# Value transposes behind the first Q strip, and the last two attention units interleaved, in a hybrid GDN, sliding-window attention and mixture-of-experts layer

## What is computed

```python
h = x @ w_in                      # 512 x 2048 by 2048 x 5648
a_qkv, a_z, a_beta, a_dec, b_q, b_k, b_v = jnp.split(h, SPLITS, axis=-1)
o_a = gated_delta_rule(...)       # 8 GDN heads of 128
# attention: 16 query heads of 64 on 4 key/value heads; a chunk of 64 queries
# sees its own chunk of keys and the one before
s = jnp.einsum('bnqhgd,bnkhd->bhgnqk', qc, kb) * (d ** -0.5)
s = s - slopes[:, :, None, None, None] * dist
s = jnp.where(valid, s, -jnp.inf)
p = jax.nn.softmax(jnp.concatenate([s, sink], -1), axis=-1)[..., :-1]
o = jnp.einsum('bhgnqk,bnkhd->bnqhgd', p.astype(v.dtype), vb)
mix = jnp.concatenate([o_a, o_b.astype(x.dtype)], -1) @ w_o
```

## Time and profile before

| | us |
|---|---|
| median of 3 runs | 2172.26 |
| the profiled execution | 2169.26 |
| its span, first to last instruction | 2167.3 |
| TensorE busy | 1920.7 (89% of the span) |
| VectorE busy | 1179.5 (54%) |
| ScalarE busy | 583.2 (27%) |
| GpSimd busy | 397.3 (18%) |
| mean granted TensorE clock | 0.959 |

### The profile page before, as it was taken

The page is one execution under the profiler, slowest core; times in us unless marked ns, Lnnn a source line. Parts: engine busy times, 40 slices in busy tenths (PEclk is TensorE's granted clock), DMA queues, the critical chain, the costliest instruction groups (busy, mean ns, idle before and its releaser), DMA issues.

```text
span 2167.3 us, 23945 instructions
## 1 busy us (share of the span) xinstructions
PE 1920.7 (89%) x9724; PEld 1208.9 (56%) x9724; DVE 1179.5 (54%) x1808; ACT 583.2 (27%) x875; POOL 397.3 (18%) x301
## 2 busy tenths in 40 slices
PE   4799999999999899699979998988998899898981
PEld 3687877787787777588853443433333333343330
DVE  6676577567657255411365554545555454454558
ACT  4233224224314255411222222122122112212211
POOL 1643233324233222144300000000000000000002
PEclk9899999999999999799979999999999999999995
DMA  5421222122113121152679999999999999999981
GB/s 194 155 78 40 59 59 59 42 57 66 52 40 85 52 66 59 64 181 97 238 267 403 403 405 407 411 398 403 406 415 408 398 414 402 398 413 404 412 352 78
DMA packets 170847, 505.89 MB, mean 233 GB/s; under 512 B 16336, under 2 KB 108624, under 8 KB 117232
## 3 DMA queue, kind: packets, MB, share of 16 engines
q1 hardware_dynamic: 167552, 491.61, 59.6%
q0 software_dynamic: 2608, 8.53, 1.4%
q10 hardware_dynamic: 576, 4.19, 0.5%
HBM read 499.97 MB, written 12.71 MB: 237 GB/s over the span
## 4 chain that ended last, share of the span: by engine, by line
PE 47%; DMA 33%; DVE 14%; ACT 2%; issue 2%; POOL 1%; SPq 1%; DVEq 0%; ACTq 0%
DMA ring<-in_w_up 32%; PE bank L1646 8%; PE bank L2004 8%; PE bank L1648 8%; PE bank L1647 8%; PE bank L2013 3%; PE bank L1777 2%; PE bank L1774 2%; PE bank L1766 2%; DVE half L1128 2%; PE bank L1973 1%; DVE gd_L L1249 1%; DVE att L1306 1%; DVE sc L1301 1%; DVE sc L1318 1%
## 5 line engine op out<-in xcount | busy, mean ns | idle before, releaser
L2004 PE MATMUL bank<-ring,xbT 128*64 128x512 f32 x2048 | 484.6, 616 | 78.8 <-DMA ring<-in_w_up 76.6
L599 POOL TENSOR_TENSOR wlo<-raw,whi 128x512 fp32r<-128x512 f32 x244 | 341.0, 1431 | 636.8 <-ACT whi L710 413.9
L1517 DVE TENSOR_TENSOR r<-r,bank 128x512 f32<-128x512 f32 x512 | 318.0, 681 | 211.1 <-PE bank L1973 210.6
L2004 PEld LDWEIGHTS bank<-ring,xbT 128*64 128x64 f32 x2048 | 156.8, 141 | 360.5 <-issue 358.3
L1646 PE MATMUL bank<-hTh,wlo 128*128 128x512 f32 x720 | 306.3, 425 | 21.9 <-POOL wlo L599 21.9
L1648 PE MATMUL bank<-hTh,whi 128*128 128x512 f32 x720 | 283.8, 394 | 0.0
L1647 PE MATMUL bank<-hTl,whi 128*128 128x512 f32 x720 | 283.3, 393 | 0.0
L987 ACT ACTIVATE yw<-bank,wts_all 64x512 f32<-64x512 f32 x256 | 174.8, 683 | 252.8 <-PE bank L2013 248.8
L2013 PE MATMUL bank<-ring,hidT 128*64 128x512 f32 x1024 | 228.5, 599 | 0.5 <-ACT hidT L980 0.5
L646 POOL DMA_INDIRECT xb<-h_scr,idx_tok x32 | 29.8, 931 | 885.6 <-PE bank L1980 871.7
L1973 PE MATMUL bank<-yhl,place 128*128 128x512 f32 x512 | 158.9, 430 | 11.9 <-DVE r L1517 9.1
(11 more groups left out here) (312 smaller groups left out, 2163.1 us busy)
## 6 DMA issues: line engine op xcount, KB each, us to landing
ring<-in_w_gate SPq DMA_DIRECT2D x128, 1024.0 KB, 28.4
ring<-in_w_up SPq DMA_DIRECT2D x128, 1024.0 KB, 29.0
ring<-in_w_down SPq DMA_DIRECT2D x128, 1024.0 KB, 28.2
raw<-in_w_in SPq DMA_DIRECT2D x45, 1024.0 KB, 5.6
raw<-in_w_o SPq DMA_DIRECT2D x16, 1024.0 KB, 5.2
xt<-in_x SPq DMA_DIRECT2D x4, 1024.0 KB, 9.3
h_scr<-xt SPq DMA_DIRECT2D x4, 1024.0 KB, 7.6
r<-h_scr SPq DMA_DIRECT2D x1, 4096.0 KB, 13.7
```

The source lines that it names most:

```text
L599: i = pool.tensor_tensor(wlo[sl][:, part, :], raw[sl][:, :].rearrange("p (k n) -> p k n", k=KD)[:, part, :], whi[sl][:, part, :].bitcast(F ...
L1517: dve.tensor_tensor(v, v, comb_bank(q, tt)[:, :], ALU.add).then_inc(comb_done, 1)
L2004: i = mm(GU[SLOTS * h:SLOTS * (h + 1), :], xT_[:, k, :], w[:, kk * F:(kk + 1) * F], start=k == 0, stop=k == KD - 1)
```

## The change

Two places.

**The head.** TensorE runs the first query strip (`k_steps(Q0, ...)`) ahead of the eight value transposes instead of behind them; the second strip stays behind them.

**The tail.** The functions of a unit are cut into pieces. Units 0 to 5 call them in the old order. Unit 7 gets its own score buffer `sc_last` (in the last 8 KB of `hTl`, so DVE waits for the last strip's matmuls, `strip_mm`), its own `att8_last`, and for r = 0 the banks `PA[0]`, `PA[1]`, which no strip needs any more. So TensorE issues both units' scores, and DVE and ACT take the first half of unit 7 between unit 6's exponentials and its normalisation. New waits: unit 7's scores of r = 1 wait until DVE has read unit 6's from the same bank (`sc_step`), and unit 6's value product, which writes `B2`, waits until DVE has read unit 7's scores there. The value product of every unit also names `at_out`. On ACT the split of block 0 moves from between the units to ahead of both.

```diff
@@ -190,6 +190,8 @@
+        sc_last = at("sc_last", HT + 56 * KB, [P, 2, 2, 2, 2 * P])
+        att8_last = at("att8_last", ATT + 28 * KB, [P, 5, 8])
...
@@ -456,6 +458,19 @@
+        UNITS = 8
+
+        def sc_of(u):
+            return sc_last if u == UNITS - 1 else sc
+
+        def att8_of(u):
+            return att8_last if u == UNITS - 1 else att8
+
+        def score_bank(u, r, tp):
+            if r == 0:
+                return PA[tp] if u == UNITS - 1 else [B0, B1][tp]
+            return [B2, BM][tp]
+
...
@@ -858,24 +873,33 @@
-            def attend(m, j):
-
-                u = 2 * m + j
-                for r in range(2):
...
-                                           accum_out=att8[:, 2, 4 * r + t:4 * r + t + 1])
-                i.then_inc(pexp, 1)
+            def exps(u, r):
+                j, a8 = u % 2, att8_of(u)
+                act.wait_ge(nmx, 2 * u + (r + 1))
...
+                if r == 1:
+                    i.then_inc(pexp, 1)
+
+            def turned(u):
                 for i in range(4):
                     act.wait_ge(pt_ps, 4 * u + (i + 1))
+            def mixed(u):
                 act.wait_ge(at_ps, u + 1)
-                act.activation(mixT[:, bass.ds(u + HEADS, 1), :].rearrange("p o s -> p (o s)"), B2[:, :],
-                               ACT.Copy).then_inc(at_out, 1)
+                act.activation(mixT[:, u + HEADS, :], B2[:, :], ACT.Copy).then_inc(at_out, 1)
+
+            def attend(m, j):
+                u = 2 * m + j
+                for r in range(2):
+                    exps(u, r)
+                turned(u)
+                mixed(u)
 
...
@@ -907,11 +931,17 @@
-            attend(3, 0)
             act.wait_ge(strip_mm, STRIPS)
             act.wait_ge(at_out, 4)
             split_mix(0)
-            attend(3, 1)
+            exps(6, 0)
+            exps(6, 1)
+            exps(7, 0)
+            turned(6)
+            exps(7, 1)
+            mixed(6)
+            turned(7)
+            mixed(7)
             for i in range(1, 3):
...
@@ -1285,49 +1315,59 @@
-            def attend(m, j):
-
-                u = 2 * m + j
-                if j == 0:
-                    W(dve, at_ps, 2 * m)
-                    dve.tensor_copy(kg[:, :], kdup[:, bass.ds(m, 1), :].rearrange("p o s -> p (o s)"))
-                    dve.tensor_copy(vg[:, :, :], vtok[:, :, bass.ds(m * HD, HD)])
-                    dve.tensor_copy(sl[:, :, :], attn_small[:, :].rearrange("p (a h) -> p a h", a=2)[:, :, bass.ds(m * 4, 4)]).then_inc(at_small, 1)
+            def group(m):
                 dve.wait_ge(at_small, m + 1)
-                W(dve, pt_ps, 4 * u)
-                for r in range(2):
-                    for tp in range(2):
-                        dve.wait_ge(sc_ps, 4 * u + (2 * r + tp + 1))
-                        dve.scalar_tensor_tensor(out=sc[:, r, tp, :, :], in0=dist[:, tp:tp + 2, :],
-                                                 scalar=sl[:, 0, 2 * j + r:2 * j + r + 1],
-                                                 in1=[[B0, B1], [B2, BM]][r][tp][:, :].rearrange("p (a b) -> p a b", a=2),
...
+
+            def biased(u, r):
+                j, a8 = u % 2, att8_of(u)
+                if r == 0 and u < UNITS - 1:
+                    W(dve, pt_ps, 4 * u)
+                for tp in range(2):
+                    dve.wait_ge(sc_ps, 4 * u + (2 * r + tp + 1))
+                    dve.scalar_tensor_tensor(out=sc_of(u)[:, r, tp, :, :], in0=dist[:, tp:tp + 2, :],
+                                             scalar=sl[:, 0, 2 * j + r:2 * j + r + 1],
+                                             in1=score_bank(u, r, tp)[:, :].rearrange("p (a b) -> p a b", a=2),
...
+            def normed(u):
+                a8 = att8_of(u)
                 dve.wait_ge(pexp, u + 1)
-                dve.tensor_tensor(att8[:, 4, :], att8[:, 2, :], att8[:, 3, :], ALU.add).then_inc(inv_sum, 1)
...
+                dve.reciprocal(a8[:, 4, :], a8[:, 4, :]).then_inc(inv_sum, 1)
                 dve.wait_ge(inv_sum, 2 * u + 2)
                 for r in range(2):
                     for tp in range(2):
-                        dve.tensor_tensor(sc[:, r, tp, :, :], sc[:, r, tp, :, :],
-                                          att8[:, 4, c:c + 2].rearrange("p (a o) -> p a o", o=1).broadcast_to([P, 2, 2 * P]),
+                        dve.tensor_tensor(sc_of(u)[:, r, tp, :, :], sc_of(u)[:, r, tp, :, :],
+                                          a8[:, 4, c:c + 2].rearrange("p (a o) -> p a o", o=1).broadcast_to([P, 2, 2 * P]),
                                           ALU.mult).then_inc(pn, 1)
...
-            attend(0, 0)
-            attend(0, 1)
-            for m in range(1, 3):
-                attend(m, 0)
-                attend(m, 1)
-            attend(3, 0)
-            attend(3, 1)
+            for u in range(UNITS - 2):
+                if u % 2 == 0:
+                    group(u // 2)
+                biased(u, 0)
+                biased(u, 1)
+                normed(u)
+            group(3)
+            biased(6, 0)
+            biased(6, 1)
+            dve.wait_ge(strip_mm, STRIPS)
+            biased(7, 0)
+            normed(6)
+            biased(7, 1)
+            normed(7)
...
@@ -1811,44 +1851,59 @@
+            k_steps(Q0, slot(0), 0, KD)
             for j in range(2):
                 pe.wait_ge(strip_out, Q0 - 1 + j)
                 pe.wait_ge(o_done, HEADS)
                 for t in range(TT):
                     i = pe.transpose([B0, B1][j][:, t * P:(t + 1) * P], vT[:, j, t * P:(t + 1) * P], ident)
                 i.then_inc(v_T, 1)
-            for j in range(2):
-                k_steps(Q0 + j, slot(j), 0, KD)
-
-            def attend(m, j, feed):
-                u = 2 * m + j
-
-                pe.wait_ge(at_small, m + 1)
+            k_steps(Q0 + 1, slot(1), 0, KD)
+
+            def scores(u):
+                j = u % 2
+                pe.wait_ge(at_small, u // 2 + 1)
                 pe.wait_ge(strip_out, u + (Q0 + 1))
-                W(pe, at_out, u)
+                if u < UNITS - 1:
+                    W(pe, at_out, u)
                 for r in range(2):
                     q0, q1 = HD * r, HD * (r + 1)
                     for tp in range(2):
+                        if u == UNITS - 1 and r == 1:
+                            pe.wait_ge(sc_step, 8 * (u - 1) + (5 + 2 * tp))
                         for t in (2 * tp, 2 * tp + 1):
-                            i = mm([[B0, B1], [B2, BM]][r][tp][:, (t % 2) * 2 * P:(t % 2 + 1) * 2 * P],
+                            i = mm(score_bank(u, r, tp)[:, (t % 2) * 2 * P:(t % 2 + 1) * 2 * P],
                                    aq[j][q0:q1, t * P:(t + 1) * P], kg[q0:q1, t * P:(t + 2) * P], start=True, stop=True)
                         i.then_inc(sc_ps, 1)
-                feed(13)
+
+            def turn(u):
                 for r in range(2):
                     pe.wait_ge(pn, 4 * u + (2 * r + 2))
                     for g in range(2):
                         for t in range(TT):
...
-                feed(2)
+
+            def weigh(u):
                 pe.wait_ge(pt, 4 * u + 4)
+                if u == UNITS - 2:
+                    pe.wait_ge(sc_step, 8 * (u + 1) + 5)
+                W(pe, at_out, u)
                 for t in range(TT):
                     for g in ((0, 1) if t else (1,)):
                         for r in range(2):
...
+
+            def attend(m, j, feed):
+                u = 2 * m + j
+                scores(u)
+                feed(13)
+                turn(u)
+                feed(2)
+                weigh(u)
                 feed(KD)
...
@@ -1866,8 +1921,11 @@
-            for j in range(2):
-                attend(3, j, lambda n: None)
+            for u in (6, 7):
+                scores(u)
+            for u in (6, 7):
+                turn(u)
+                weigh(u)
```

More of the change, by code:

```diff
@@ L859, in _ @@
             iteration(HEADS, last=True)
+            def exps(u, r):
+                j, a8 = u % 2, att8_of(u)
+                act.wait_ge(nmx, 2 * u + (r + 1))
+                act.activation(a8[:, 3, 4 * r:4 * r + 4], a8[:, 1, 4 * r:4 * r + 4], ACT.Exp,
+                               bias=sl[:, 1, 2 * j + r:2 * j + r + 1])
+                for t in range(TT):
+                    v = sc_of(u)[:, r, t // 2, t % 2, :]
+                    i = act.activation(v, v, ACT.Exp, bias=a8[:, 1, 4 * r + t:4 * r + t + 1],
+                                       accum_out=a8[:, 2, 4 * r + t:4 * r + t + 1])
+                if r == 1:
+                    i.then_inc(pexp, 1)
+            def turned(u):
+                for i in range(4):
+                    act.wait_ge(pt_ps, 4 * u + (i + 1))
+                    act.activation(pT[:, i, :], [BS, BO, B0, B1][i][:, :], ACT.Copy).then_inc(pt, 1)
+            def mixed(u):
+                act.wait_ge(at_ps, u + 1)
+                act.activation(mixT[:, u + HEADS, :], B2[:, :], ACT.Copy).then_inc(at_out, 1)
             def attend(m, j):
@@ new lines, in group @@
```

(18 more changed lines are left out.)

19 lines of the change are left out of this document (1 added, 18 removed).

## The result

The changed kernel took 2149.08 us (median of 4 runs, 2148.18 to 2151.27) beside 2171.72 for the kernel before (4 runs, 2169.8 to 2172.45). The profiled execution took 2148.52, its span 2146.5.

What follows compares the result with a forecast made beforehand. TensorE holds 47% of the chain, DMA 33%, VectorE 14%; TensorE idles at head and tail. Head 8.3 plus tail 8.9 is 17.2 us: 2169.26 becomes 2152.1, plus 3.0 to the median gives 2155.1, range 2150.5 to 2160.

Steps and rivals of the forecast that it cites:

- the head: From the last GDN matmul to unit 0's scores: TensorE goes straight on, scores at 750.3 instead of 758.64, 8.3 us gained.
- The covers: At the head, time to spare before TensorE needs its inputs: 7.7 us (copies, queries), 3.6 (second strip), about 6 (third strip).
- the chain of the two units: Tail, units 6 and 7: unit 7's transposes at 887.9 instead of 896.84, 8.9 us earlier.
- the projection's cold start: Output projection's first 4.0 us at half rate, worth 2.0 us; taken as unchanged, possibly 0.5 better to 1.5 worse.
- the first rival: Tail: full clock returns in unit 6 and stays, the projection starts warm; 4.4 us more, 2150.7 us; chance 0.13.
- the base: Profiled execution of the kernel before, 2169.26 us, from which the gain was subtracted; the median of its runs lies 3.0 above.
- The sum: Head 8.3 plus tail 8.9 us, 17.2 us gained; chance 0.72.
- the failed step: Tail, unit 7's transposes to the output projection: unchanged at 8.31 us, if the clock is at half as before.
- The other rivals: Head's gain absorbed, 2163.4 us (0.10); projection stays at half clock, 2191 (0.03); expert DMAs start at their own time, 2172.3 (0.02).
- The rule on transposes: Skill's claim that transposes don't engage full clock; by it unit 7's chain stays at half clock and the gain at 17.2 us.

Runs made afterwards that it cites:

- the second profile: The changed kernel once more, unaltered, against the kernel before: 2151.09 us (median of 5 runs), ratio 0.9908.
- fillers: Extra matmuls, results unused: 30 after the scores of units 6 and 7 each in the kernel before, 2165.23 us; 33 in the changed kernel, 2149.74 and 2148.35 us.

## Why the prediction was right and where it failed

**Right: the head.** "8.3 us" for unit 0's scores was 8.35. That it fits to 0.1 is partly luck: against the four profiles with the old head the same gain is 7.6 to 8.5, by how long the clock stayed at half there. The clock stayed full, as taken. The covers were there: queries at 742.1 (742.6 forecast), the third strip's split over at 746.7 (747), both before 749.97.

**Right: the chain of the two units.** From DVE's first step of unit 6 to unit 7's transposes 19.35 us, forecast 887.9 − 868.20 = 19.7. The split of block 0 was hidden: ACT's first exponential still waited 0.36 us for DVE, forecast 0.3. Unit 6's transposes came 11.07 us after DVE's first step (11.3), and the extra semaphores cost nothing that shows (109.54 us between the head and unit 6, 109.56 before).

**Failed: "From there on nothing changes: 905.15 − 896.84 = 8.31 us to the output projection, if the clock is at half as before", and with it the projection's cold start, "I take it as it was".** In two of three profiles the section took 5.48 us and the projection began warm, 2.83 + 1.85 = 4.7 us less. This is the first rival, put at 4.4 us and given a chance of 0.13. The argument against it was that the clock had stayed at half between 896.84 and 909.1 "although TensorE was mostly busy". That stretch began with a clock already down, after an idle of 8.53 us; in the changed kernel the two units' bursts are 2.17 us apart, and in those two profiles the clock that had returned behind unit 6's transposes was still there. The short gap alone does not secure it: in the second profile, with a gap of 2.37 us, the clock fell again at 881, and 7.38 us went by to a cold projection. What does secure it is work in the gaps: with fillers in both units the clock stayed at 1.00 in all three profiles. Why one execution keeps the clock and the next does not stays open. The row for the return, 881.8 in the earlier trace rows, had been read, and the step was still carried over from the old kernel.

**Also mis-sized: the base.** The sum was made against one execution whose tail was 2.9 us shorter than that of the next profile, because its clock came back earlier (881.7 instead of 911). The 3.0 us from that profile to the median were carried over to the changed kernel as a constant. The changed kernel's profile lies only 0.6 us under its own median (1.4 under that of the ten runs). Part of the 3.0 was perhaps half-clock work in unit 6 that the change hides; the executions without a profile cannot show it.

**How the miss adds up.** Forecast 2155.1, measured 2149.1, 6.0 us. Up to the first expert load the profile gained 22.66 where the sum had 17.2: 4.7 are the clock of the failed step, 0.4 the chain (9.29 for 8.9), 0.3 the stretch before the head. The longer expert stage took back 1.9. The base gave 3.0 − 0.6 = 2.4. Rounded, that is the 6.0. The lower end of the range, 2150.5, stood only 0.2 under the rival's 2150.7, so that any further gain beside the rival left it.

**The other rivals** did not occur: the head alone gave 9.0 us, so it was not absorbed; the first load followed the projection; and the projection was at full clock from its start or from 4.4 us on.

**The rule on transposes.** At 881.8, before, the clock rose during unit 6's transposes, and TensorE had done nothing else since 878.68; at 874.7, after, it rose 0.4 us behind them. The Trainium skill (TensorE: Matmul & The Clock Gate, section on PE-mode transposes) says that full rate "doesn't engage" for transposes; by it neither rise was to be expected. The traces disagree: unit 7's sixteen took 2.30 us at a granted clock of 1.00, unit 6's at half 3.68. The page measured bf16, these are fp32.

## What to carry to other kernels

A stretch in which two engines hand work back and forth can be paid twice on TensorE: the idle, and the half clock behind it (here 8.2 and 5.0 to 5.8 us). When a change closes the gaps, price the matmuls behind them at both clock levels and ask whether what was cold is still on the chain. Take two or three profiles of the kernel before where the clock moves inside the part that changes; one is a draw. And a term of 2 to 3 us that the rows show every time can vanish in a single comparison of times if a later stage varies by 3.
